# Zero products in TensorE's early waits, context tiles behind a later gate, weight splits one block earlier and at step ends: one core of Trainium2

## What is computed

```python
u  = rms_norm(h,  norm_w[l]) * (1.0 + scale[:, None, :]) + shift[:, None, :]   # 512 tokens
uc = rms_norm(hc, norm_w[l]) * (1.0 + scale_c) + shift_c                       # 256 context rows
p = u @ w_in[l]                        # q, k, v, za, glu (a and g), zc
k_c, v_c = kv_heads(uc @ w_in[l][:, K_LO:V_HI], k_norm_w[l])
attn = attend_blocked(q, k_all, v_all) * jax.nn.silu(p[..., ZA_LO:ZA_HI])
conv = conformer_conv(p[..., GLU_LO:GLU_HI], ...) * jax.nn.silu(p[..., ZC_LO:ZC_HI])
out = jnp.concatenate([attn, conv], axis=-1) @ w_out[l]
h = h + gate[:, None, :] * out
```

## Time and profile before

| | |
|---|---|
| median of 3 runs | 1129.38 us (1126.33 to 1129.78) |
| profiled execution, its own time | 1131.45 us |
| its span, first to last instruction | 1129.5 us |
| mean granted clock of TensorE | 0.986 of full speed |
| busy: TensorE / DVE / ACT / POOL | 1073.8 / 644.1 / 443.7 / 12.1 us |
| TensorE's share of the chain that ended last | 82% |
| DVE's and ACT's shares of it | 9% and 4% |

### The profile page before, as it was taken

One profiled execution on the slowest core, in us unless ns is written; L12 is line 12 of the kernel. 1 busy time (PEld: TensorE's weight loads), 2 busy tenths in 40 slices (PEclk: granted clock), 3 DMA queues, 4 the chain that ended last, 5 costly groups with the idle time before them and its releaser, 6 DMA issues.

```text
span 1129.5 us, 22451 instructions
## 1 busy us (share of the span) xinstructions
PE 1073.8 (95%) x9774; PEld 833.7 (74%) x9774; DVE 644.1 (57%) x1004; ACT 443.7 (39%) x724; POOL 12.1 (1%) x13
## 2 busy tenths in 40 slices
PE   5979999897999999999999989999999999999998
PEld 3767776766687777777777766687888888888887
DVE  4568899947348584758585736755444223444232
ACT  4353454668334642433334123444343112333211
POOL 0000000000000000000000000000000000000000
PEclk8999999999999999999999999999999999999999
DMA  9812223100223210101101040032233232222330
GB/s 366 329 57 75 75 75 131 57 1 1 92 114 131 75 57 21 35 26 40 40 21 39 3 187 4 20 106 93 91 99 97 93 98 89 93 94 95 111 103 28
DMA packets 26161, 94.98 MB, mean 84 GB/s; under 512 B 2897, under 2 KB 3153, under 8 KB 25553
## 3 DMA queue, kind: packets, MB, share of 16 engines
q1 hardware_dynamic: 26064, 93.54, 24.2%
HBM read 89.34 MB, written 4.19 MB: 83 GB/s over the span
## 4 chain that ended last, share of the span: by engine, by line
PE 82%; DVE 9%; ACT 4%; issue 3%; DMA 1%; SPq 0%; POOL 0%; DVEq 0%; ACTq 0%
PE psum L800 20%; PE psum L801 19%; PE psum L802 19%; PE psum L810 5%; PE psum L1180 3%; DVE work L1863 2%; PE psum L975 2%; PE psum L932 2%; PE psum L1011 1%; PE psum L1193 1%; PE psum L1148 1%; PE psum L1252 1%; PE psum L1229 1%; DMA work<-weights 1%; DVE small_temps L2045 1%
## 5 line engine op out<-in xcount | busy, mean ns | idle before, releaser
L1919 DVE TENSOR_TENSOR weights_low<-ring,weights_high 128x1024 fp32r<-128x1024 f32 x72 | 88.2, 1225 | 75.2 <-ACT weights_high L1515 75.2
L1515 ACT ACTIVATE weights_high<-ring 128x1024 fp32r<-128x1024 f32 x72 | 75.8, 1053 | 128.8 <-PE psum L802 127.6
L800 PE MATMUL psum<-normed_high,weights_high 128*128 128x512 f32 x256 | 101.5, 397 | 0.1
L802 PE MATMUL psum<-normed_high,weights_low 128*128 128x512 f32 x256 | 101.1, 395 | 0.0
L801 PE MATMUL psum<-normed_low,weights_high 128*128 128x512 f32 x256 | 101.1, 395 | 0.0
L801 PE MATMUL psum<-hidden_low,weights_high 128*128 128x512 f32 x256 | 99.6, 389 | 0.0
L802 PE MATMUL psum<-hidden_high,weights_low 128*128 128x512 f32 x256 | 99.6, 389 | 0.0
L800 PE MATMUL psum<-hidden_high,weights_high 128*128 128x512 f32 x256 | 99.6, 389 | 0.0
L1485 ACT ACTIVATE work<-psum 128x384 f32<-128x384 f32 (+2 forms) x124 | 58.6, 515 | 76.4 <-PE psum L932 27.0
L1863 DVE SCALAR_TENSOR_TENSOR work<-work,small_sb 128x512 f32<-128x512 f32 x116 | 79.7, 742 | 0.0
L800 PE MATMUL psum<-pair_normed_high,pair_weights_high 128*128 128x512 f32 x176 | 76.8, 436 | 0.8 <-DVE normed_low L1923 0.8
(11 more groups left out here) (278 smaller groups left out, 2117.1 us busy)
## 6 DMA issues: line engine op xcount, KB each, us to landing
ring<-weights SPq DMA_DIRECT2D x135, 512.0 KB, 3.6
work<-weights SPq DMA_DIRECT2D x10, 512.0 KB, 13.2
residual<-xT SPq DMA_DIRECT2D x4, 512.0 KB, 5.8
mixed<-weights SPq DMA_DIRECT2D x4, 512.0 KB, 7.3
residual_saved<-residual SPq DMA_DIRECT2D x8, 256.0 KB, 4.2
residual<-residual_saved SPq DMA_DIRECT2D x1, 2048.0 KB, 9.1
outT<-residual SPq DMA_DIRECT2D x8, 256.0 KB, 3.2
tables_sb<-tables SPq DMA_DIRECT2D x1, 1280.0 KB, 11.3
```

The source lines that it names most:

```text
L800: pe.matmul(out, wh, high(k), start=first and n == 0, stop=False)
L802: ins = pe.matmul(out, wl, high(k), start=False, stop=last and n == len(order) - 1)
L1515: act.activation(wsplit(q)[0], room_of(b), ACT.Copy).then_inc(w_high, 1)
L1919: vec.tensor_tensor(low, room_of(b), high.bitcast(F32), ALU.subtract).then_inc(w_low, 1)
```

## The change

Five things, in the diff below. (1) POOL clears the tile `QW` first, and TensorE multiplies zeros from it into PSUM bank 3 (`filler`): 16 products ahead of `x_sum`, two, two and three ahead of the turns of tiles 0, 1 and 2, and four behind each of the first two turns. (2) The context tiles are scaled on DVE four behind a2 and four behind g2, and shifted on ACT behind g2, no longer behind g1. (3) The splits of blocks k (8) and v (9) are issued beside blocks 5 and 6 rather than 6 and 7, the low part of v at the end of block 6. (4) Six taps fewer stand beside the first eight blocks, so that 35 rather than 29 are left for attention. (5) The first two blocks of the out projection are split one a step, at u = 15 and 16, on DVE at the step's end.

```diff
-IN_TAPS = [0, 0, 2, 3, 4, 3, 5, 4] + [8, 9, 6, 4, 4, 4, 3] + [4] * 5 + [5, 3]
+IN_TAPS = [0, 0, 2, 3, 3, 2, 3, 2] + [8, 9, 6, 4, 4, 4, 3] + [4] * 5 + [5, 3]
...
+FILLER_BANK = 3
+BEFORE_SUMS = 16
+BEFORE_TURN = {0: 2, 1: 2, 2: 3}
+BEHIND_TURN = 4
...
-SPLIT_OUT = 14
+SPLIT_OUT = 15
...
 def split_beside(n):
-    if n <= OWN_BUFFERS:
-        return {1: [OWN_BUFFERS], 2: [OWN_BUFFERS + 1]}.get(n, []) + [n + 2] * (n == OWN_BUFFERS)
+    if n < OWN_BUFFERS + 2:
+        return {1: [OWN_BUFFERS], 2: [OWN_BUFFERS + 1], 5: [OWN_BUFFERS + 2], 6: [OWN_BUFFERS + 3]}.get(n, [])
     return [n + 2] * (n + 2 < len(IN_BLOCKS))
...
+            pool.memset(QW[:], 0.0).then_inc(filler_ready, 1)
             pool.memset(SILU[:], 0.0).then_inc(zeroed, 1)
...
+            def filler(n):
+                for _ in range(n):
+                    pe.matmul(psum[:, FILLER_BANK * S:FILLER_BANK * S + P], QW[:, 0:P], QW[:, 0:P], start=True, stop=True)
...
             def modulated_turn(k):
                 if k >= DK:
                     return
+                filler(BEFORE_TURN.get(k, 0))
                 pe.wait_ge(*is_free(f"m{k}"))
...
+            pe.wait_ge(filler_ready, 1)
+            filler(BEFORE_SUMS)
             pe.wait_ge(tables_in, 16)
             sum_over("x_sum", lambda j: SQ1[:, 2 * j, :], DK // 2, S, each=(x_pairs, 1))
             pe.wait_ge(c_ready, 1)
             for k in range(2):
                 modulated(k)
                 modulated_turn(k)
+                filler(BEHIND_TURN)
...
-                if x == "g1":
+                if x == "g2":
                     for k in range(DK):
                         act.wait_ge(ctx_scaled, k + 1)
...
-                if u == SPLIT_OUT:
-                    for m in range(2):
-                        weights_high(SPLIT_AT["out0"] + m)
+                if u in (SPLIT_OUT, SPLIT_OUT + 1):
+                    weights_high(SPLIT_AT["out0"] + u - SPLIT_OUT)
...
+                behind = split_beside(n) if n == OWN_BUFFERS else []
                 for q in split_beside(n):
-                    weights_low(q)
+                    if q not in behind:
+                        weights_low(q)
...
-                if x == "a1":
-                    context_scaled(0, DK)
...
+                if x in ("a2", "g2"):
+                    half = "ag".index(x[0]) * DK // 2
+                    context_scaled(half, half + DK // 2)
                 taps = convolve_on(taps, more)
+                for q in behind:
+                    weights_low(q)
```

More of the change, by code:

```diff
@@ L592, in build @@
         zeroed = sem("zeroed")
+        filler_ready = sem("filler_zeroed")
         negmax, probs_scaled = sem("negmax_ready"), sem("probs_scaled")
@@ L2100, in _ @@
                     modulation_columns("gate", 2, "b_gate")
-                if u in (SPLIT_OUT, SPLIT_OUT + 1):
-                    weights_low(SPLIT_AT["out0"] + u - SPLIT_OUT)
                 if u in (12, 13):
@@ L2114, in _ @@
                         denominator(f"conv{n}")
+                if u in (SPLIT_OUT, SPLIT_OUT + 1):
+                    weights_low(SPLIT_AT["out0"] + u - SPLIT_OUT)
             def gated_low(n):
```

## The result

The changed kernel took 1111.8 us (median of four runs, 1111.7 to 1112.23), the kernel before 1128.55 in the same session (1126.33 to 1129.78): a ratio of 0.9857, 95% interval 0.9843 to 0.987, faster by 1.4%. The forecast was 1115.0 with a range of 1110.5 to 1121.5. The profiled execution took 1111.7 us, its span 1109.7, against 1131.45 and 1129.5: 19.8 us less. The profile of before was taken from a run 2.9 us above its median, that of the changed kernel at its median.

What follows compares the result with a forecast made beforehand. TensorE (PE) bounds the kernel, so gains lie only in its waits and half-clock stretches. -3.1 - 7.7 - 2.4 + 1.8 - 4.2 = -15.6 from 1131.45 gives 1115.9, by the median 1113.8; forecast 1115.0, range 1110.5 to 1121.5.

Steps and rivals of the forecast that it cites:

- (1) The start: First 30 us: products of zeros hold the clock until weights bound PE; modulation 4 begins at 28.05, not 31.16; gain 3.1.
- the rule of the Trainium skill: Start: a throttled stretch costs its length times one minus the granted ratio, giving back 5.15 us rather than 3.1.
- The 16 products ahead of the sums: Start: these fillers stand in PE's idle 8.16 us before x_sum, and ending a little late costs nothing.
- (2) to (4) Block k: Stage 2: block k starts at 78.5, not 84.78, its half-clock stretch goes, kc's sum comes at 91.35, not 99.03; gain 7.7.
- the new wait ahead of the first head sum: Stage 2, behind kc: PE waits 1.2 us for ACT, which ends kx's squares at 88.7 while kc ended at 87.6.
- zc3: Block zc3: PE's wait for its low part falls from 1.95 to 1.2 us and the clock holds; gain 2.4.
- Attention: Attention: six more taps and an addition delay DVE's row maxima, so the scores of step 8 come later; loss 1.8.
- (5) Step 15: Attention, step 15: the 2.54 us wait ahead of value product 12 and the half clock behind it go; gain 4.2.
- The products do hold the clock: Answers the rival that fillers at the start don't hold the clock: total -10.1, 1121 us; chance 0.12.
- DVE doesn't bound stage 2: Answers the rival that DVE bounds stage 2, giving 4.7 instead of 7.7 + 2.4: 1121 us; chance 0.13.
- the clock didn't fall elsewhere: Answers the rival that new waits or the start bring one or two 3.5 us half-clock stretches: 1117 to 1118.5; chance 0.15.
- the last two rivals: Whole kernel: slower, from PE standing at kc until ACT's last shift (0.02); no net change, 1129 us (0.03).

Runs made afterwards that it cites:

- part 5 alone: Kernel before with only the first two out projection blocks split at steps 15 and 16, on DVE at the step's end: 1124.34 us (0.9965).
- 62 products: Changed kernel with 31 more products of zeros, of 4 columns each, ahead of the 16 before the square sums: 1124.61 us (0.9962).
- narrow products: 31 products of zeros of 4 columns instead of 128: 1113.39 us on the changed kernel; added to the kernel before, 1124.32 us.

## Why the prediction was right, and where it wasn't

**The total.** Right to 3.2 us, though not by its own sum alone, and so in part by luck. Measured against the profile of before the sum of the touched places is 1.88 + 9.55 + 2.15 = 13.6, where I had 15.6; the stretch from 640 us on, which I had at nothing, gave 5.25 in the profiles and some 4 in the medians. An error of omission made good for a start that I had put too high.

**(1) The start** is the term that was mis-sized. Put at 3.1, it measured 1.88 between the two profiles. Part of that was luck: without products modulation 4 begins at 31.16, 30.61, 30.64 and 29.84 us in four kernels, with wide ones at 29.20 to 30.14 in seven. The means are 30.56 and 29.59, so 1.0 us. The medians give 1.6 to 2.0 for the clock. The mechanism was right: the clock holds, and the arrival of weights bounds what it gives (PE waits 1.19 us for modulation 3's weights). So the rule of the Trainium skill (TensorE: Matmul & The Clock Gate, Terms) that I had weighed, 5.15 us, was further off still. Two steps in it failed. The 16 products ahead of the sums take part in nothing that counts: without them the time is the same. And the sums' 5.43 us were not paced by DVE alone: in before their first five records start 0.85 to 0.99 us apart with no wait between them, the last four 0.43 to 0.44, so that PE was the slow one. The price of a product, put at 0.28 to 0.51 us, measured 0.22 to 0.43.

**(2) to (4) Block k.** The wait of 6.67 us became 0.50 (0.6 forecast), block k came 6.18 us earlier beyond the start (6.28), the new wait ahead of the first head sum was 0.83 (1.2), the sum for kc 7.58 us earlier (7.7). The context's place and the taps each lose a good part of this when taken back; the earlier splits were never taken back alone, so what they give is not shown. The half-clock stretch is gone.

**zc3.** The wait went from 1.95 to 1.33 (1.2 forecast), no stretch at half clock followed, and the stage gained 1.97 (2.4).

**Attention.** The loss up to step 8 was 2.09 us (1.8 forecast), a third of it by the way that I wrote and the rest by another. The wait for exponentials behind late row maxima grew by 0.74 us, all at the scores of step 3 (1.78 to 2.52). At step 7 PE did not wait for exponentials as I had it: it waited 1.44 us for the bank that `gated_heads(0)` frees, which stands behind five taps and an addition on DVE. The same lateness of DVE, at its other outlet. I had searched for what the taps delay and stopped at the first thing. The size was near by luck.

**(5) Step 15.** 4.24 us in the changed kernel, 4.30 alone; 4.2 forecast.

**The rivals.** The products do hold the clock; DVE doesn't bound stage 2 (the gain is 9.55, not 4.7, and the same with and without the products); the clock didn't fall elsewhere. The chances themselves don't quite add up: what is left beside the last two rivals is 0.95, not 0.94. The rival that was real had not been named: that instructions moved by the change meet their supply at another place.

## What to carry to other kernels

Read the waits with no releaser ("issue") over the whole span before forecasting, and count the instructions that an edit adds ahead of them: in this kernel 31 products almost without work gave 4 us, as much as a stall removed elsewhere, and 62 brought the waits back. Where work is moved off one engine ahead of a split, look at the other engine's part of the same work: DVE's wait behind ACT's eight shifts (2.12 us) was longer than the four scalings added on DVE itself (1.6). And when taps or other filling work has to go somewhere, try it spread thinner: four taps a step instead of five gave 4.3 us, more than the six taps cost.

## What the runs showed of the hardware

- TensorE's waits for instructions follow the count of instructions ahead of them. At the turns near 667 us they are there with 0 and 62 added products, not with 15, 23 or 31; with 62 (248 records) they stand exactly 256 records further on. Packets of 16.3 KB bring them, and one of these came only amid a reload of 2 MB when PE had stopped for it (2.12 us, then 3.4 us at half clock). A stop of 1.59 us at the same place (part 5 alone) and one of 1.69 us (62 products) had no half clock behind them. The 31 narrow products were worth 3.8 to 4.2 us of the median. The runs of the kernel before spread from 1124.7 to 1135.0 us and those of the changed one, only four, from 1111.7 to 1112.2; with narrow products it was 1111.9 to 1117.7. What sets the spread stays open.
- A product of zeros is two records. From 1.3 us on they start 0.21 us apart, with 4 columns as with 128, and later 0.11 apart: from 7.2 us on in the changed kernel, from 19.2 us on in that with 62. Around the turns, from 14 us on, a set of four takes 1.03 us with 4 columns and 1.14 with 128.
- The column of the granted clock shows 1.00 from the start on in every kernel here. Yet the eight records of the square sums take 6.73 us back to back behind the narrow products and 3.60 in the kernel with 62 products (0.45 each). In the first, as in before, with none ahead and with eight, the first records of the sums start 0.85 us or more apart; behind 16 wide products, whose own records had gone from 0.21 to 0.11 us apart, the two records of a part start 0.50 to 0.54 apart. I read the slower pace as half clock at the start that the column doesn't show. In the changed kernel it ends at 7.2 us, and it cost nothing that the time shows.
